# Two attentions in one Trainium2 kernel: where TensorE computes its dense fillers within a round

## What is computed

```
def swa_sink_attention(q, k, v, sinks):           # first attention: 16 heads, 4 key heads, blocks of 128
    scores = einsum(qb, kk) * HEAD_DIM ** -0.5     # a block of queries against its own and the last block
    e = exp(where(valid, scores, -inf) - m)
    probs = e / (sum(e) + exp(sink - m))
    return einsum(probs, vv)

h = h + (o * silu(gate)) @ out_w                   # "ao": the attention's output projection
h = h + sigmoid(rms_norm(h) @ gate_w) * (p @ proj_w)   # "pp": p @ proj_w, independent of the attention

m_out = rms_norm(mlstm(...)) * sigmoid(mo)         # "mg": the norm's scale, spread over the head by a product
o = g0 * o_compressed + g1 * o_selected + g2 * o_window   # second attention, 8 heads: branches c, s, w
x = x + concat([m_out, a_out]) @ w_out             # "wo": the first half of its rows needs m_out alone
```

## Time and profile before

| | |
|---|---|
| median of 3 runs | 1393.8 us |
| lowest, highest | 1392.76, 1395.24 us |
| the profiled execution, its own time | 1393.03 us |
| its span | 1391.0 us |
| first attention, from about | 594 to 661 us |
| second attention, from about | 930 to 1031 us |

### The profile page before, as it was taken

The page is one execution under the profiler, slowest core; times in us unless marked ns, Lnnn a source line. Parts: engine busy times, 40 slices in busy tenths (PEclk is TensorE's granted clock), DMA queues, the critical chain, the costliest instruction groups (busy, mean ns, idle before and its releaser), DMA issues.

```text
span 1391.0 us, 17826 instructions
## 1 busy us (share of the span) xinstructions
PE 1352.9 (97%) x6632; PEld 1064.4 (77%) x6632; DVE 828.1 (60%) x1414; ACT 679.2 (49%) x1130; POOL 530.3 (38%) x259
## 2 busy tenths in 40 slices
PE   8999999999999999989999999999999999999997
PEld 6777777777778878857888887766667788888886
DVE  5576464657577754675576513378745654544666
ACT  7744635736366543585465412356545323232463
POOL 3553554635420034456100434136532655555300
PEclk9999999999999999999999999999999999999999
DMA  5221222222133323211333233130013233332331
GB/s 190 91 76 59 83 73 76 81 72 76 48 107 102 93 78 91 75 47 47 91 91 122 91 121 122 31 121 10 22 31 92 91 98 99 91 105 92 121 106 61
DMA packets 33220, 117.31 MB, mean 84 GB/s; under 512 B 3948, under 2 KB 4332, under 8 KB 32880
## 3 DMA queue, kind: packets, MB, share of 16 engines
q1 hardware_dynamic: 31976, 111.85, 25.7%
q10 hardware_dynamic: 1160, 4.34, 0.9%
HBM read 114.08 MB, written 2.10 MB: 84 GB/s over the span
## 4 chain that ended last, share of the span: by engine, by line
PE 87%; DVE 5%; ACT 3%; issue 2%; DMA 1%; POOL 1%; ACTq 0%; DVEq 0%
PE bank L1286 84%; PE bank L1741 1%; PE bank L1583 1%; DMA h<-in_xT 1%; ACT wsh L852 1%; POOL arena L762 0%; PE bank L1459 0%; POOL wsl L704 0%; DVE arena L1982 0%; PE bank L1494 0%; DVE arena L2274 0%; DMA ring<-in_wstream 0%; DVE arena L1902 0%; DVE arena L2188 0%; DVE wsl L1798 0%
## 5 line engine op out<-in xcount | busy, mean ns | idle before, releaser
L704 POOL TENSOR_TENSOR wsl<-ring,wsh 128x1024 fp32r<-128x1024 f32 x144 | 351.9, 2444 | 556.3 <-ACT wsh L852 556.2
L852 ACT ACTIVATE wsh<-ring 128x1024 fp32r<-128x1024 f32 x199 | 210.5, 1058 | 458.5 <-PE bank L1286 434.9
L1286 PE MATMUL bank<-parts1h,wsh 128*128 128x512 f32 (+1 forms) x736 | 291.8, 396 | 8.9 <-POOL wsl L704 3.4
L1286 PE MATMUL bank<-parts1h,wsl 128*128 128x512 f32 (+1 forms) x736 | 285.2, 388 | 0.0
L1286 PE MATMUL bank<-parts1l,wsh 128*128 128x512 f32 (+1 forms) x736 | 285.1, 387 | 0.0
L1286 PE MATMUL bank<-parts0h,wsh 128*128 128x512 f32 x704 | 281.2, 399 | 3.9 <-issue 1.3
L1286 PE MATMUL bank<-parts0h,wsl 128*128 128x512 f32 x704 | 274.5, 390 | 0.0
L1286 PE MATMUL bank<-parts0l,wsh 128*128 128x512 f32 x704 | 274.2, 389 | 0.0
L1286 PEld LDWEIGHTS bank<-parts1h,wsh 128*128 128x128 f32 x736 | 138.2, 188 | 46.3 <-issue 7.8
L1286 PEld LDWEIGHTS bank<-parts0h,wsh 128*128 128x128 f32 x704 | 132.1, 188 | 41.6 <-issue 10.8
L1286 PEld LDWEIGHTS bank<-parts1h,wsl 128*128 128x128 f32 x736 | 138.2, 188 | 28.9
(11 more groups left out here) (318 smaller groups left out, 1795.9 us busy)
## 6 DMA issues: line engine op xcount, KB each, us to landing
ring<-in_wstream SPq DMA_DIRECT2D x206, 512.0 KB, 3.6
arena<-in_alibi ACTq DMA_DIRECT2D x2, 1024.0 KB, 6.1
outT<-arena SPq DMA_DIRECT2D x8, 256.0 KB, 2.8
h<-in_xT SPq DMA_DIRECT2D x2, 256.0 KB, 5.6
h<-in_xT ACTq DMA_DIRECT2D x2, 256.0 KB, 6.1
h<-in_xT SPq DMA_DIRECT2D x1, 512.0 KB, 8.1
h<-in_xT ACTq DMA_DIRECT2D x1, 512.0 KB, 9.2
arena<-in_frow ACTq DMA_DIRECT2D x1, 512.0 KB, 3.4
```

Of the source, the lines that this page charges most:

```text
L704: return nc.gpsimd.tensor_tensor(dst, src, hi.bitcast(F32), ALU.subtract)
L852: nc.scalar.activation(wsh[n % NSET][:, :], src, ACT.Copy).then_inc(*done("high", ("high", L)))
L1286: return nc.tensor.matmul(*args, **kw)
```

## The change

One line of `filled` changes. The TensorE part of a filler moves from before V to behind it, in every filled round of both attentions; with it the `("F", ...)` entries of these steps are gone from the list, and each filler stands once, behind V, for all engines.

```diff
     def filled(parts, x, order, between):
 
         res = []
         for y in parts:
             extra = between.get(order.index(y[1:]), []) if y[0] == x + "V" else []
-            res += [("F", *z) for z in extra] + [y] + extra
+            res += [y] + extra
         return res
```

## The result

| kernel | median us | lowest to highest | runs |
|---|---|---|---|
| before | 1394.21 | 1392.76 to 1395.24 | 5 |
| changed | 1399.62 | 1398.23 to 1401.23 | 5 |

The ratio is 1.0039, with a 95% interval of 1.0028 to 1.0051: +5.4 us, where +4.3 was forecast, and 1399.62 us, where 1398.1 was. The profiled execution's span is 1396.4 us, against 1391.0.

A forecast was written before the change was run, and what follows sets the result against it. TensorE, busy 97% of the span, was taken as the bound. 0.5 + 0.55 + 2.97 - 1.5 + 1.8 = +4.3 us on the profiled 1393.03 gives 1397.3, or 1398.1 against the median; range 1395.3 to 1401.8.

The forecast's parts named there:

- Scoreless rounds: Rounds (2,3), (3,2), (3,3) and 18: nothing left between T and V, so V waits for copies; +2.97 us together.
- (0,3): First attention, round (0,3): ScalarE's copy is late, so V waits where the filler began; +0.5 us.
- The other scored rounds I cost at nothing: S covers the copies: Remaining filled rounds with scores: copies end within S; 0 us, up to 0.5 us each if not.
- Round 16: Second attention: round 15's filler leaves ScalarE a weight rounding that now delays round 16's copy and V; +0.55 us.
- Handovers: Dense matmul to transpose takes 0.23 us, to V 0.32; 17 fillers gain 0.09 each, -1.5 us.
- The other neighbours of a filler keep their spacing: Part of the handover term: spacings other than from filler to V or transpose stay unchanged.
- Bounded by 0 and 0.09: Limits in us put on the handover gain per filler; the upper one was taken.
- `mg` 1: Second attention, round 0: product behind V ends near 938.9 us, VectorE wants it at 937.13; +1.8 us, bounds 0 and 2.7.
- Rival (a): `mg` 1 runs at full clock and ends by 937.13 us, VectorE loses little: +2.5, 1396.3 us; chance 0.22.
- Rival (b): Clock falls to 1.2 GHz in the first attention's scoreless rounds or round 18: 3.5 us more, 1401.6 us; chance 0.13.
- The rule cited there: Short idle times between matmul groups can make the clock swing, so new waits cost more than their length; outside the sum.
- nothing downstream gives it back: Behind both attentions TensorE goes straight into dense products, so the added time stays.

The follow-up runs named there:

- e2: Changed kernel with the fillers of the four scoreless rounds (three in the first attention, round 18 in the second) ahead of V again: 1398.15 us, ratio 1.0021.
- e3: Changed kernel with the `mg` fillers and those of the four scoreless rounds ahead of V again: 1395.41 us, ratio 1.0005.
- e7: Changed kernel, fillers of scoreless rounds, `mg` and round 15 ahead of V; other engines' follow-up behind the next T in the first attention only: 1392.62 us, ratio 0.9987.
- e4: Kernel before with only `mg` 1 moved behind V, in the first round of the second attention: 1396.74 us, ratio 1.0014.
- r3: Changed kernel profiled a third time, unaltered; no median given, its profiled span +8.96 us against the first profile of before.
- r1: Changed kernel run a second time, unaltered: 1401.57 us, ratio 1.0043.
- e5: Changed kernel with the other engines' follow-up of all fillers behind V issued later, behind the next T: 1411.16 us, ratio 1.0116.
- e1: Changed kernel with `mg` 1 to 3 ahead of V again: 1401.53 us, ratio 1.0047.
- e6: Changed kernel, fillers of scoreless rounds, `mg` and round 15 ahead of V; the others' follow-up on other engines behind the next T: 1397.74 us, ratio 1.0021.

## Why the prediction was right, and where it was not

The mechanism was the one forecast: the filler covered the copies, and without it V waits. The sum was right in part because errors cancelled, and that it came so near is in part luck. By its steps:

- **Scoreless rounds, forecast +2.97: right.** Net of the handover, 0.09, the forecast is +0.40 in (2,3), +0.96 in (3,2) and +0.85 in round 18; from one T to the next those rounds are 0.49, 1.02 and 0.86 us longer. e2 takes 1.86 us out of the first attention (forecast for its three rounds: 2.03 - 0.27 = 1.76), e3 0.89 out of the second.
- **(0,3), forecast +0.5: right** (a wait of 0.63, the round 0.54 longer). "The other scored rounds I cost at nothing: S covers the copies" **failed twice**. In (1,2) ScalarE has the rounding and the `pp` copy of the neighbour's filler ahead of its own, and V waits 0.33. In round 15 S lasts 0.72 us, VectorE's copy 0.68 and starts 0.10 after S does, and V waits 0.22.
- **Round 16, forecast +0.55: right in size** (a wait of 0.61, the round 0.51 longer). What the step lacked is what the lateness does next: V of round 17 waits 1.62 instead of 1.31. With the filler of round 15 ahead of V all of 15, 16 and 17 are back (e7: 0.00). The last rounds were forecast at about +1.3 net of handovers and measured +1.96 at full clock.
- **Handovers, forecast 0.09 a filler: the mechanism right, the size low.** A transpose follows a filler by 0.23 us, as taken (647.77 to 648.00). "The other neighbours of a filler keep their spacing" **failed**: T itself is shorter behind a filler, 1.03 us instead of 1.09, and S comes 0.06 sooner. Where nothing waits, rounds (1,3) and (2,2), the gain is 0.15 a filler. On average it is 0.10 in the first attention, where some T and V still wait a little (e7: 0.68 for seven), and 0.16 in the second (0.78 for five). "Bounded by 0 and 0.09" was wrong.
- **`mg` 1, forecast +1.8: right in kind, too large.** VectorE's idle time was 1.78 us in e4 and r3, 1.18 and 0.89 in the other profiles of the change, by how much of V and `mg` fell into the half clock. The cost is less than the idle time, +1.37, +1.12, +1.13 and +0.19, because VectorE's next instruction gets shorter (last section). Rival (a) comes close in r1 only, and not by its condition: `mg` 1 was at half clock there.
- **The clock. Rival (b) took place in two of three profiles.** The last rounds cost about 2.8 us more in r1 and r3 than in the first profile, where the rival had 3.5. With round 15's filler behind V, four of seven profiles show a fall between 1024 and 1048 us (r1, r3, e2, e5); with it ahead, none of six. The forecast left it out of the sum at a chance of 0.13, which was too little by these profiles; the longest wait ahead of it is 1.62 us now, not the 1.31 that had stayed at full clock. The rule cited there (the Trainium skill, TensorE: Matmul & The Clock Gate, "A second HAM failure mode: psum-queue depth-cycling") said that short idle times can make the clock swing; these runs agree for some executions and not for others. The clock is not the whole loss: at the same mean granted clock, 0.996, two runs of the changed kernel took 1398.23 and 1398.73 us, and eight of the kernel before 1392.42 to 1395.03.
- **Ahead of the change, forecast 0, measured +0.8 to +1.5.** No step of the prediction makes it, and no wait does: TensorE waits 2.48 us at 86 us in either kernel, and runs on at the upper level in before and at the lower in the changed one. First before, then after:

```profile
85.87 0.63 PE L1459 MATMUL bank<-con,arena 128*128 128x128 f32 x4 [2.48 <-ACT arena L831]
86.25 0.48 PE L1286 MATMUL bank<-parts1h,parts1l 128*128 128x512 f32 x1
```

```profile
85.79 1.09 PE L1459 MATMUL bank<-con,arena 128*128 128x128 f32 x4 [2.48 <-ACT arena L831]
86.53 0.78 PE L1286 MATMUL bank<-parts1h,parts1l 128*128 128x512 f32 x1
```

All seven profiles of five kernels (changed, e1, e2, e5, e7) have this fall and none of six of four kernels (before, e3, e4, e6). So in the profiles it goes with the kernel rather than with the execution, though the kernels don't differ up to there; whether the other timed runs follow this is not shown. Why stays open. Over three profiles each this stretch is +1.21 and -0.21 us on average: by them 1.4 us, about a quarter of the measured +5.4, is no wait of a moved instruction or of its neighbours.

So the sum held by cancelling: 0.33 + 0.22 + 0.31 = 0.9 us of waits in (1,2), 15 and 17 were left out, while the handovers gave some 0.6 more than the -1.5 forecast (ten at 0.10 and seven at 0.16) and `mg` cost 0.7 less in the first profile. That profile's +4.35 over the attentions meets the forecast; r1's and r3's, with the clock's fall, are +6.2 and +7.2. And the measured +5.4 holds the stretch ahead of the change, which the forecast had at 0. The claim that nothing downstream gives it back held between the attentions (-0.06 to -0.34, which before itself shows too).

## What to carry to other kernels

A filler earns its place by the wait that it covers: before moving one, find for each round which copy, on which engine, ends between its two neighbours, and what the neighbour's filler puts ahead of that copy in the same queue. The best order here is not one rule for all rounds: ahead of the values where no scores stand in between or where they are too short to cover the copy (round 15), behind them elsewhere (handovers are cheaper, 0.10 to 0.16 us each), and a product that another, busier engine waits for stays as early as it can. When a change is worth 0.4%, cut the span at named instructions and compare stretch by stretch over several profiles; the stretch ahead of the change tells how much of the difference is not its own.

## What the runs showed of the hardware that was not expected

**The granted clock falls in single places of some microseconds, and what that costs depends on who sets the pace.** After equal waits (2.48 us at 86 us; 1.62 us near 1028) it fell in some profiles and not in others. It cost about 2.8 us in rounds 18 and 19, and 0.1 us at 937 us, where VectorE is the bound.

**VectorE and GpSimd take turns.** VectorE's second product behind `mg` (L2372) lasts 0.69 us in one profile and 1.58 in another. First GpSimd, then VectorE, in the first profile of the change, in r3 and in r1:

```profile
942.48 1.27 POOL L704 TENSOR_TENSOR parts0l<-arena,parts0h 128x512 fp32r<-128x512 f32 x1
942.72 1.58 DVE L2372 SCALAR_TENSOR_TENSOR arena<-arena 128x512 f32<-128x512 f32 x1
```

```profile
941.52 1.26 POOL L704 TENSOR_TENSOR parts0l<-arena,parts0h 128x512 fp32r<-128x512 f32 x1
942.38 0.96 DVE L2372 SCALAR_TENSOR_TENSOR arena<-arena 128x512 f32<-128x512 f32 x1
```

```profile
942.27 1.77 POOL L704 TENSOR_TENSOR parts0l<-arena,parts0h 128x512 fp32r<-128x512 f32 x1
942.23 0.69 DVE L2372 SCALAR_TENSOR_TENSOR arena<-arena 128x512 f32<-128x512 f32 x1
```

Where GpSimd started first, VectorE ends 0.55 us after it (943.75 to 944.30; 942.78 to 943.34), however long it had been under way; where VectorE started first, by 0.04 us, it takes 0.69 and GpSimd 0.5 longer. Hence the cost of `mg` 1 in the changed kernel: idle time of 1.18 us against an L2372 of 1.58, as before (+1.13); 1.78 against 0.96 (+1.12); 0.89 against 0.69, which leaves 0.2 (+0.19) unexplained.

e6 and e7 show it with GpSimd's work beside VectorE and without. In round 3 e6 holds back the follow-up of `mh` 3, and GpSimd's part of it runs beside a small product of VectorE (L2439; L713 is L704 above), which lasts 1.12 us. In e7 GpSimd is idle there, and the same product lasts 0.17: the 0.95 us by which e6's rounds 0 to 4 are longer. First GpSimd and VectorE in e6, then VectorE in e7:

```profile
951.81 1.27 POOL L713 TENSOR_TENSOR parts0l<-arena,parts0h 128x512 fp32r<-128x512 f32 x1 [1.99 <-ACT parts0h L1220]
951.98 1.12 DVE L2439 TENSOR_TENSOR small<-small,gat 128x8 f32<-128x8 f32 x1
```

```profile
953.69 0.17 DVE L2439 TENSOR_TENSOR small<-small,gat 128x8 f32<-128x8 f32 x1
```

The Trainium skill (SBUF — State Buffer, "Who interferes with whom") says that these two engines share a pair of ports under an exclusive lock; these rows agree.
